# Seven of eleven down chunks of the later feed-forward stages in the seven-product form, kept banks summed by adding transfers

## The reference, cut to what matters

```python
def swiglu(h, w_gate, w_up, w_down):
    return (jax.nn.silu(h @ w_gate) * (h @ w_up)) @ w_down

for layer in range(2):
    x = x + 0.5 * swiglu(rmsnorm(x, ...), gate[layer, 0], up[layer, 0], down[layer, 0])
    ...                                   # mixer, cross attention
    x = x + 0.5 * swiglu(rmsnorm(x, ...), gate[layer, 1], up[layer, 1], down[layer, 1])
```

## Time and profile before

| | us |
|---|---|
| median of 3 runs | 1182.55 (1182.21 to 1182.57) |
| the profiled execution | 1182.64 |
| its span, first to last instruction | 1180.7 |
| PE busy | 1173.8 |
| DVE busy | 944.4 |
| ACT busy | 688.1 |
| POOL busy | 105.0 |

### The profile page before, as it was taken

One profiled execution on the slowest core, in us unless ns is written; L12 is line 12 of the kernel. 1 busy time (PEld: TensorE's weight loads), 2 busy tenths in 40 slices (PEclk: granted clock), 3 DMA queues, 4 the chain that ended last, 5 costly groups with the idle time before them and its releaser, 6 DMA issues.

```text
span 1180.7 us, 17445 instructions
## 1 busy us (share of the span) xinstructions
PE 1173.8 (99%) x6787; PEld 1025.7 (87%) x6787; DVE 944.4 (80%) x1102; ACT 688.1 (58%) x925; POOL 105.0 (9%) x97
## 2 busy tenths in 40 slices
PE   9999999999999999999999999999999999999998
PEld 8888889889989888888888888889887898888886
DVE  6687897875657689888978988997887676798887
ACT  7566556853557566555565655564576556565553
POOL 1010001420142010000010000010012121000000
PEclk9999999999999999999999999999999999999999
DMA  9966755454344465665655656547623435666561
GB/s 319 334 205 197 204 188 179 144 182 141 141 145 176 143 197 162 212 212 181 202 189 177 208 185 205 185 143 214 212 92 127 144 114 166 203 217 198 191 195 55
DMA packets 164013, 214.93 MB, mean 182 GB/s; under 512 B 14832, under 2 KB 139120, under 8 KB 163824
## 3 DMA queue, kind: packets, MB, share of 16 engines
q1 hardware_dynamic: 163664, 213.30, 56.2%
q0 software_dynamic: 144, 0.52, 0.1%
q10 hardware_dynamic: 144, 0.26, 0.1%
HBM read 213.02 MB, written 1.05 MB: 181 GB/s over the span
## 4 chain that ended last, share of the span: by engine, by line
PE 98%; DMA 1%; ACT 0%; POOL 0%; DVE 0%; SPq 0%; issue 0%; POOLq 0%; DVEq 0%
PE ps L2302 30%; PE ps L2309 16%; PE ps L2281 15%; PE ps L2282 15%; PE ps L2283 15%; PE ps L2385 1%; PE ps L2572 1%; PE ps L3036 1%; PE ps L2892 1%; DMA arena<-in_first 1%; PE ps L3059 0%; PE ps L2580 0%; PE ps L2997 0%; PE ps L2994 0%; PE ps L2453 0%; PE ps L2644 0%
## 5 line engine op out<-in xcount | busy, mean ns | idle before, releaser
L2302 PE MATMUL ps<-hT,w_parts 128*128 128x512 f32 x1568 | 375.4, 391 | 0.3 <-issue 0.2
L2302 PEld LDWEIGHTS ps<-hT,w_parts 128*128 128x128 f32 x1568 | 289.8, 188 | 59.6 <-issue 1.5
L1355 DVE TENSOR_TENSOR w_parts<-raw,w_parts 128x2048 fp32r<-128x2048 f32 x85 | 196.2, 2317 | 58.0 <-ACT w_parts L749 57.9
L2309 PEld LDWEIGHTS ps<-hT,w_parts 128*128 128x128 f32 x1568 | 201.4, 191 | 8.0 <-DVE w_parts L1431 0.2
L884 ACT ACTIVATE w_parts<-raw 128x2048 fp32r<-128x2048 f32 x108 | 206.1, 1908 | 0.6 <-DMA raw<-in_ffn_w_gate 0.6
L749 ACT ACTIVATE w_parts<-raw 128x2048 fp32r<-128x2048 f32 x85 | 162.4, 1920 | 73.5 <-PE ps L2283 70.5
L2309 PE MATMUL ps<-hT,w_parts 128*128 128x256 f32 x1568 | 204.1, 283 | 0.0
L1571 DVE TENSOR_TENSOR w_parts<-raw,w_parts 128x2048 fp32r<-128x2048 f32 x45 | 103.0, 2289 | 14.3 <-ACT w_parts L884 14.3
L2281 PE MATMUL ps<-w_parts,arena_r 128*128 128x512 f32 (+1 forms) x264 | 102.8, 389 | 0.0
L2282 PE MATMUL ps<-w_parts,arena_r 128*128 128x512 f32 (+1 forms) x264 | 102.8, 389 | 0.0
L2283 PE MATMUL ps<-w_parts,arena_r 128*128 128x512 f32 (+1 forms) x264 | 102.3, 387 | 0.0
(11 more groups left out here) (373 smaller groups left out, 1975.1 us busy)
## 6 DMA issues: line engine op xcount, KB each, us to landing
raw<-in_ffn_w_down SPq DMA_DIRECT2D x44, 1024.0 KB, 5.0
raw<-in_ffn_w_gate SPq DMA_DIRECT2D x43, 1024.0 KB, 5.4
raw<-in_ffn_w_up SPq DMA_DIRECT2D x43, 1024.0 KB, 5.4
raw<-in_xattn_wkv SPq DMA_DIRECT2D x16, 1024.0 KB, 5.4
raw<-in_even_w_in SPq DMA_DIRECT2D x13, 1024.0 KB, 5.2
raw<-in_xattn_wq SPq DMA_DIRECT2D x8, 1024.0 KB, 5.1
raw<-in_xattn_wo SPq DMA_DIRECT2D x8, 1024.0 KB, 5.4
raw<-in_odd_w_in SPq DMA_DIRECT2D x6, 1024.0 KB, 5.6
```

What stands on the lines that cost most here:

```text
L1355: ins = V.tensor_tensor(lo, src, hi.bitcast(F32), ALU.subtract)
L2302: mm(ps[:, bank0 + m, :], cols(w_hi, n, k, CW, m * P, (m + 1) * P), hT[:, k, :, :].rearrange("p a c -> p (a c)"), start=k == 0, stop=False)
L2309: last = mm(ps[:, bank0 + m, SEQ:], cols(w_lo, n, k, CW, m * P, (m + 1) * P), hT[:, k, 0, :], start=False, stop=k == KT - 1)
```

## The change

In the later stages seven of the eleven down chunks are in the seven-product form, those of hidden blocks 1, 2, 3 and 5, 6, 7, 8 (a run of three and a run of four). Blocks 4, 9 and 0, 10 stay plain. DVE reads the four banks no more. ACT copies them each time into two fixed buffers (`Mixed.copied`), and POOL issues a transfer from SBUF to SBUF that adds the copy to the kept buffer (`accum_op=ALU.add`), two of 512 KB for each chunk but the first of a stage. ACT waits for the transfer before it copies into the same buffer again. At the end of the stage DVE waits for the last two transfers (`kept_added_in`) after `gate_scale(10)`, and only then makes the first two `kept_sum`; before, those two stood ahead of `gate_sum(10)`. Three semaphores of POOL are merged into one (`pool_set`).

```diff
@@ class Mixed
-            FIRST, COUNT = (2, 0, 0, 0), (3, 5, 5, 5)
+            FIRST, COUNT = (2, 0, 0, 0), (3, 7, 7, 7)
+            copied = [part(at_, [2, 512]) for at_ in (10240, 4992)]
@@ ACT turn(j, between, mixed, out, added)
+                    if out is not None:
+                        act.wait_ge(mixed_mm[f], mixed_mm_at(f, out) + 1)
+                        if added and (f > 1 or not isinstance(out, int) or out > 1):
+                            act.wait_ge(kept_added_in[0], kept_added_at(f, out))
+                        nc.scalar.activation((Mixed.copied if added else Mixed.kept[f])[0], ps[:, 0:2, :],
+                                             ACT.Copy).then_inc(mixed_read[f], 1)
                     act.wait_ge(chunks_used, j * 3 + (base + 2))
...
                     hidden(j + (f * FJ + 1), gu_hi)
+                    if out is not None:
+                        if added and (f > 1 or not isinstance(out, int) or out > 1):
+                            act.wait_ge(kept_added_in[1], kept_added_at(f, out))
+                        nc.scalar.activation((Mixed.copied if added else Mixed.kept[f])[1], ps[:, 2:4, :],
+                                             ACT.Copy).then_inc(mixed_read[f], 1)
@@ ACT ffn, f > 0
-                    turn(2, mixed=1, first_out=0)
-                    turn(3)
-                    with act.Fori(2, mixed_end(f)) as i:
-                        turn(i * 2, mixed=i)
-                        turn(i * 2 + 1)
+                    turn(2, mixed=1, out=0)
+                    turn(3, mixed=2, out=1, added=True)
+                    turn(4, out=2, added=True)
+                    turn(5, mixed=3)
+                    with act.Fori(4, 7) as i:
+                        turn(i + 2, mixed=i, out=i - 1, added=True)
+                    turn(9, out=6, added=True)
@@ DVE ffn, f > 0
                     turn_mixed(1, 0)
-                    turn_mixed_next(2, 1)
-                    turn_read(3, 1)
-                    with dve.Fori(2, mixed_end(f)) as i:
-                        turn_mixed(i * 2, i)
-                        turn_read(i * 2 + 1, i)
+                    with dve.Fori(1, 3) as i:
+                        turn_mixed_next(i + 1, i)
+                    turn(4)
+                    turn_mixed(5, 3)
+                    with dve.Fori(4, 7) as i:
+                        turn_mixed_next(i + 2, i)
+                    turn(9)
                 made[0] = base + FFN_CHUNKS - 1
-                kept_sum(0, 2, 0)
-                kept_sum(1, 3, 2)
+                if f == 0:
+                    kept_sum(0, 2, 0)
+                    kept_sum(1, 3, 2)
                 gate_sum(FJ - 1)
                 gate_scale(FJ - 1)
+                if f:
+                    for half in range(2):
+                        dve.wait_ge(kept_added_in[half], kept_added_at(f, mixed_end(f)))
+                    kept_sum(0, 2, 0)
+                    kept_sum(1, 3, 2)
@@ POOL
+            def ffn(f):
+                for i in range(1, Mixed.COUNT[f]):
+                    for half in range(2):
+                        pool.wait_ge(mixed_read[f], mixed_read_at(f, i) + half + 1)
+                        if f > 1 or i > 1:
+                            pool.wait_ge(kept_added_in[half], kept_added_at(f, i))
+                        pool.dma_start(Mixed.kept[f][half], Mixed.copied[half],
+                                       accum_op=ALU.add).then_inc(kept_added_in[half], 16)
@@ PE ffn
                     turn(2, False, mixed=0)
-                    turn(3, False, kept=1, mixed=1)
-                with pe.Fori(2, mixed_end(f)) as i:
-                    turn(i * 2, False, kept=i)
-                    turn(i * 2 + 1, False, mixed=i)
+                    with pe.Fori(1, 3) as i:
+                        turn(i + 2, False, kept=i, mixed=i)
+                if f:
+                    turn(5, False, kept=3)
+                    turn(6, False, mixed=3)
+                    with pe.Fori(4, 7) as i:
+                        turn(i + 3, False, kept=i, mixed=i)
+                else:
+                    with pe.Fori(2, mixed_end(f)) as i:
+                        turn(i * 2, False, kept=i)
+                        turn(i * 2 + 1, False, mixed=i)
                 turn(FJ - 1, False, held=f == 3, kept=mixed_end(f))
@@ semaphores
-            G.memset(neg_half[:, :], -0.5).then_inc(neg_half_set, 1)
-            pool.wait_ge(neg_half_set, 1)
+            G.memset(neg_half[:, :], -0.5).then_inc(pool_set, 1)
+            pool.wait_ge(pool_set, 1)
```

More of the change, by code:

```diff
@@ L451, in build @@
                             for i in range(2))
-            kept = [[part(at_, [2, 512]) for at_ in (10240, 4992)], kept_later, kept_later, kept_later]
+            copied = [part(at_, [2, 512]) for at_ in (10240, 4992)]
+            kept = [copied, kept_later, kept_later, kept_later]
         class Even:
@@ L510, in build, with kept_added_at @@
         mixed_read = [quarter_in[0]] + [es["kz_done"]] * 3
+        kept_added_in = [sem(f"kept_added_in{half}") for half in range(2)]
+        def kept_added_at(f, i):
+            return ((f - 1) * (Mixed.COUNT[f] - 1) + i - 1) * 16
         def mixed_end(f):
@@ L516, in counted @@
         def counted(f, i, each, first, extra=0):
-            return (i - Mixed.FIRST[f]) * each + (1 + (f - 1) * (5 * each + extra) if f else first)
+            return (i - Mixed.FIRST[f]) * each + (1 + (f - 1) * (Mixed.COUNT[f] * each + extra) if f else first)
         def w_sums_at(f, i):
@@ L877, in hidden, with turn @@
                                          ACT.Copy).then_inc(gu_hi_done, 1)
-                def turn(j, between=lambda c: None, mixed=None, first_out=None):
+                def turn(j, between=lambda c: None, mixed=None, out=None, added=False):
                     def split(m):
@@ L895, in sums_hi @@
                         nc.scalar.activation(Mixed.w_hi, Mixed.w_sums, ACT.Copy).then_inc(w_sums_hi[f], 1)
-                    if mixed is not None and first_out is None:
+                    if mixed is not None and out is None:
                         sums_hi()
-                    if first_out is not None:
-                        act.wait_ge(mixed_mm[f], mixed_mm_at(f, first_out) + 1)
-                        nc.scalar.activation(Mixed.kept[f][0], ps[:, 0:2, :], ACT.Copy).then_inc(mixed_read[f], 1)
+                    if out is not None:
[4 more added lines that the diff above has]
+                                             ACT.Copy).then_inc(mixed_read[f], 1)
                     act.wait_ge(chunks_used, j * 3 + (base + 2))
@@ L906, in turn @@
                     hidden(j + (f * FJ + 1), gu_hi)
-                    if first_out is not None:
-                        nc.scalar.activation(Mixed.kept[f][1], ps[:, 2:4, :], ACT.Copy).then_inc(mixed_read[f], 1)
-                    if mixed is not None and first_out is not None:
+                    if out is not None:
[3 more added lines that the diff above has]
+                                             ACT.Copy).then_inc(mixed_read[f], 1)
+                    if mixed is not None and out is not None:
                         sums_hi()
@@ L945, in ffn @@
                          mixed=2)
-                    turn(5, first_out=2)
+                    turn(5, out=2)
                     turn(6, mixed=3)
@@ L1290, in small_tables @@
                     nc.scalar.activation(masks[:, :], masks_f, ACT.Copy).then_inc(consts_made, 1)
-            act.wait_ge(neg_half_set, 1)
+            act.wait_ge(pool_set, 1)
             nc.scalar.activation(half_rstd[:, :], neg_half[:, 0:2], ACT.Silu)
@@ L1898, in even @@
                                     const("decayT", RET_H, P), ALU.mult).then_inc(es["s_done"], 1)
-                dve.wait_ge(es["dx_done"], 1)
+                dve.wait_ge(pool_set, 3)
                 hc = "p (h c) -> p h c"
@@ L2134, in small_tables @@
                     dve.wait_ge(consts_made, 1)
-                    dve.wait_ge(small_w_set, 1)
+                    dve.wait_ge(pool_set, 2)
                     for lo, hi, src in zip(small_w_lo, small_w_hi, small_w_k):
@@ L2271, in _ @@
                                     ALU.mult).then_inc(os_["c2_read"], 1)
+                for f in range(1, 4):
+                    if v == norm_no(f // 2, 3 * (f % 2)):
+                        ffn(f)
             last_norm()
@@ L3068, in values @@
                 last.then_inc(os_["pv_mm"], 1)
-            pe.wait_ge(neg_half_set, 1)
+            pe.wait_ge(pool_set, 1)
             for _ in range(WARM):
```

9 lines of the change are left out of this document (4 added, 5 removed).

## The result

The changed kernel takes 1210.51 us, the median of four runs (1209.60 to 1211.64), against 1182.43 (1182.21 to 1182.57): ratio 1.0238, 95% interval 1.0220 to 1.0256. It is 28.1 us slower. The forecast was 1188.3, in a range up to 1197: the direction was right, the size was not. The profiled execution took 1210.05 us with a span of 1208.3, at a granted clock of 0.991.

A forecast was written before the change was run, and what follows sets the result against it. PE, busy for 1173.8 of 1180.7 us, was taken as the bound. Terms -5.10, +1.15, +1.41 and +2.98, plus 2.4 for c and 2.85 for W, gave +5.7: 1188.3 us, range 1185 to 1194, 8 in 10 1178.5 to 1197.

The forecast's parts named there:

- Saved on PE: Later stages: six more seven-product chunks take 4.08 us off PE, the end of the late read 1.02; in all -5.10.
- run of three: Turn 4 of each later stage: DVE's lag exceeds its limit by 0.21, 0.21 and 0.31, plus a restart each: +1.15 us.
- order of the sums: Stage's end: the two first `kept_sum`, moved behind `gate_sum(10)`, stall PE before the last down chunk: +2.98 us in all.
- late read: Between turns 3 and 4, DVE's read of banks 0 and 1 costs PE 0.29 us, in stage 3 0.44; ACT's copy removes it.
- restart: After a stall of PE: another 0.14 us, because the weight loads have lost their lead.
- run of four: By turn 9 DVE's lag is 0.33 + c over its limit; with a restart, in three stages: +1.41 + 3c.
- c: Turn 5's raw down chunk: reload delay from adding transfers sharing the DMA engines, 0.8 us a stage, bounds 0 and 2.6.
- W: Stage's end: how late the last adding transfer lands, paid by DVE and PE: 0.95 us a stage, bounds 0 and 3.9.
- first rival: The transfers cost nothing: they land in time and do not delay the reload, c = W = 0; 1183.1 us, chance 0.27.
- the second: Rival: limits are looser, DVE's lag never reaches PE and half the stage-end stall is absent; 1179.0 us, chance 0.20.
- The third: Rival: DMA engines fill up if adding costs over 2.3 times a plain move; at 4 us each about 1220, chance 0.10.

The follow-up runs named there:

- e4: The changed kernel with each adding transfer moving 128 of its 1024 columns, 64 KB instead of 512 KB: 1183.12 us.
- e10: The changed kernel with POOL's pair of transfers from the end of turn 4 held until turn 5's down chunk has landed: 1200.31 us.
- e11: The changed kernel with the added waits of both e9 and e10, all bytes still moved: 1188.53 us.
- e3: The changed kernel, but DVE reads the banks itself in turns 4 and 9 and the two sums stand back ahead of `gate_sum(10)`: 1185.65 us.
- e9: The changed kernel with SP's 1 MB load at the ends of stages 1 and 2 held until the first of the last two transfers has landed: 1200.02 us.

## Why the prediction was wrong

**Saved on PE, run of three, order of the sums.** These held in the main. Between turns 3 and 4 of stage 1 PE's step is 15.94 us (465.16 to 481.10), so the late read is gone; the next step is 16.36, 0.47 too long, where 0.21 and a restart of 0.14 were forecast; in stages 2 and 3 it is 15.93 and 15.99, so 0.6 us in all stand against a forecast of 1.15. The order of the sums was measured alone at +2.6 for 2.98. That part of the sum, with the run of four at c = 0, is 1183.1, and e4 gave 1183.12; to agree so closely with terms that are off by half a microsecond is luck.

**c, the reload of the down chunk.** This is the first term that failed. The step read "I take half of the 1.6, 0.8, since the reload meets mainly the second transfer", with an upper bound of 2.6. DVE's turn 5 took 22.20, 22.69 and 23.17 us between scales; less 18.42 and the 0.23 of the later slot, c is 3.5 to 4.5, mean 4.0. Undoing it gave 10.2 us (e10), though e10 has 11 matmul steps more at half the clock, some 2.2 us, at its stages' ends. I had priced sharing, in which both streams run at a lower rate. What the traces show is mainly queueing: the up load, then the second transfer's 2.65 us, then the down load, which mix only where one gives way to the next.

**W, the landing at the stage's end.** This is the second. I forecast 0.95 with an upper bound of 3.9; DVE waited 5.79, 5.47 and 1.18 us in the three stages. The price of the transfer itself was right: 2.65 us of all engines, and 6.9 us to landing in stage 3, where no load stands between. With SP's load held back (e11) DVE waits 1.58, 0.52 and 0.85, mean 0.98, and that kernel takes 1188.53 us, beside a forecast of 1188.3. The forecast was thus near the time of this change with a free road for its transfers, but the agreement is in part luck: in e11 DVE's turn 5 takes 18.63, 18.79 and 18.38 us, so c is nought where I had 0.8 a stage, and 14 matmul steps at half the clock (2.8 us), which I had not, stand in for it. What I left out is which loads SP issues around the pair. The timeline of before had SP's issues at this place, and I read it for PE and DVE only.

**The clock.** No term had it. In the changed kernel the granted clock of 4 us stretches around the gap in stage 1 is (us, busy of PE, PEld, DVE, ACT, POOL, then the clock, DMA share, GB/s):

```profile
592.00:596.00 4.00, 2.63 (x12) 1.85 (x10) 3.90 (x6) 0.00 (x0) 0.00 (x0) 1.00 0.03 9
596.00:600.00 4.00, 0.00 (x0) 0.00 (x0) 3.88 (x6) 0.72 (x2) 0.00 (x0) 0.63 0.36 100
600.00:604.00 4.00, 3.22 (x8) 2.58 (x9) 3.48 (x3) 3.51 (x2) 0.00 (x0) 0.51 0.47 162
```

PE was idle for 6 us, and then ran at half speed, 1.2 GHz, for its first matmuls. In all 18 steps are of 0.43 (6 and 7 at the ends of stages 1 and 2, 5 behind the middle wait of stage 3), 3.6 us. A stall of PE costs more than its length. The three together are 9.7 (c, 12.1 for 2.4), 9.6 (W, 12.4 for 2.85) and 3.6; less the 0.5 by which the run of three came out cheaper they make 22.4, and the forecast was 22.2 us short.

**The rivals.** The first and the second were decided by this: where the transfers cost nothing the time is the first rival's. The third had the right engine and a wrong mechanism: it asked whether the engines have the time, and they have. Its worth is in its point, 2.3 times a plain move; the measured factor is 2.0.

The Trainium skill, "Collectives: The Full Stack", section on the bandwidth ceiling, says that such an add costs two source reads and nothing for the adding itself; 8.1% against 4.1% here agrees. By the anatomy of a transfer in the Trainium skill's "DMA: Bandwidth & Descriptors" I had estimated 3.2 us to landing; that is below every landing of this size here: 5.2 us in the median for a plain move, 6.0 for an adding one.

**Still open.** e3 is 3.0 us over the kernel before though its order of sums is the old one. Its trace, of its fastest execution (1184.01), accounts for 1.4: where DVE reads banks late (its turns 4 and 9) PE's next step between gate chunks is 16.66 to 17.09 us instead of 15.89, 6.5 us too many in six places, against the 5.1 that the prediction has as saved. The rest, up to the median, was not taken apart. In e9 PE waited 2.0 us at the end of stage 1 and 2.3 at the end of stage 3 without a drop of the clock, while in e11 two waits of 1.9 each had one; why is not known.

## What to carry to other kernels

Price a transfer in two ways: by the engines' time it takes, and by what is issued in the few us before it and behind it, on every queue. A load that someone waits for is late by all that arrived before it, so background transfers belong behind it, and a wait on the issuing side, which cost nothing here, can put them there. When a gain comes from less work on the bounding engine, check each turn of the engine next to it: here DVE had 0.7 us less room than the matmuls that were saved.

## What the runs showed of the hardware

- A transfer from SBUF to SBUF with adding takes twice the engines' time of a plain one of the same size: 8.1% against 4.1% of the span for 5328 packets.
- In the changed kernel a transfer issued by POOL 5.6 us or more after its last one has its first packet 1.9 to 2.6 us after its issue, and, at 512 KB with adding, its last at 5 to 7. A load of 1 MB that SP issued 0.6 us before the second of a pair went ahead of it almost whole: 5.5 to 6.0 and 10.3 to 11.4 us. Loads that SP issued 1.65 us or more after a transfer's issue stood in the main behind it.
- After a wait of PE of 6 us at a stage's end the granted clock was at half (1.2 GHz) for its next 6 or 7 steps, and behind some waits of 2 to 3 us too, though not behind all.
